# x laid out twice by the host, loaded turned ahead of and between the first weights, instead of transposed on TensorE

## The reference

```python
h = rmsnorm(x, norm_mix_g[l])                          # x: 1 x 256 x 1024
proj = jnp.einsum('bsd,dc->bsc', h, w_in[l])           # w_in: 1024 x 7168
u, v, bg, cg, xs, ga, gb = jnp.split(proj, split_at, axis=-1)
u = jax.nn.gelu(u, approximate=False)
v = rmsnorm(jax.nn.gelu(v, approximate=False), norm_v_g[l])
a = spatial_gating(u, v, w_s[l], b_s[l])
...
x = x + jnp.einsum('bsd,de->bse', m, w_out[l])
```

## Time and profile before

| | |
|---|---|
| median of 3 runs | 1056.23 us (1055.58 to 1056.95) |
| profiled execution | 1057.68 us, span 1055.9 us |
| TensorE busy | 1029.4 us, 97% |
| VectorE, ScalarE, GpSimd busy | 505.6, 408.0 and 22.2 us |
| moved by DMA | 327.89 MB, 311 GB/s over the span |

### The profile page before, as it was taken

One profiled execution on the slowest core, in us unless ns is written; L12 is line 12 of the kernel. 1 busy time (PEld: TensorE's weight loads), 2 busy tenths in 40 slices (PEclk: granted clock), 3 DMA queues, 4 the chain that ended last, 5 costly groups with the idle time before them and its releaser, 6 DMA issues.

```text
span 1055.9 us, 13811 instructions
## 1 busy us (share of the span) xinstructions
PE 1029.4 (97%) x5646; PEld 692.9 (66%) x5646; DVE 505.6 (48%) x713; ACT 408.0 (39%) x644; POOL 22.2 (2%) x42
## 2 busy tenths in 40 slices
PE   9999999999999999999999999999999999999985
PEld 6888878888999999898897544444444444434332
DVE  5676677987977755766665412121112121111112
ACT  6734634446444434664844222222222222212112
POOL 1000000010000000100000000000000000000000
PEclk9999999999999999899999999999999999999988
DMA  9977548976888653474255999999999999999992
GB/s 331 391 266 242 195 156 289 320 256 230 293 312 296 240 198 122 142 261 156 96 200 230 367 423 421 421 421 420 420 421 421 421 422 421 421 421 421 421 419 93
DMA packets 86467, 327.89 MB, mean 311 GB/s; under 512 B 5776, under 2 KB 5936, under 8 KB 61696
## 3 DMA queue, kind: packets, MB, share of 16 engines
q1 hardware_dynamic: 85056, 323.45, 79.3%
q0 software_dynamic: 1344, 3.50, 1.0%
HBM read 325.88 MB, written 1.05 MB: 310 GB/s over the span
## 4 chain that ended last, share of the span: by engine, by line
PE 48%; DMA 8%; DVE 1%; issue 1%; ACT 1%; DVEq 0%; ACTq 0%
PE bank L1025 18%; PE bank L1048 9%; PE bank L1061 3%; DMA raw<-in_w_expert_up 3%; DMA es<-in_w_expert_up 3%; PE bank L993 3%; DMA e_wlo<-in_w_expert_up 2%; PE bank L580 2%; PE bank L583 2%; PE bank L586 2%; PE bank L1034 1%; PE bank L550 1%; PE bank L556 1%; PE bank L553 1%; PE bank L1007 1%; PE bank L1009 1%
## 5 line engine op out<-in xcount | busy, mean ns | idle before, releaser
L1600 DVE TENSOR_TENSOR wlo<-raw,whi 128x2048 fp32r<-128x2048 f32 x87 | 199.0, 2290 | 95.9 <-ACT whi L1114 95.5
L1114 ACT ACTIVATE whi<-raw 128x2048 fp32r<-128x2048 f32 x87 | 165.9, 1912 | 95.9 <-PE bank L556 38.6
L2221 DVE SCALAR_TENSOR_TENSOR YS<-bank,wsl,gate2q 128x512 f32<-128x512 f32 x32 | 24.0, 751 | 217.6 <-PE bank L1048 217.6
L1025 PE MATMUL bank<-raw,XT 128*64 128x512 f32 x360 | 119.8, 597 | 0.0
L1025 PE MATMUL bank<-es,XT 128*64 128x512 f32 x328 | 113.9, 606 | 4.4 <-DMA es<-in_w_expert_up 3.4
L553 PE MATMUL bank<-wlo,hh 128*128 128x512 f32 x224 | 87.5, 391 | 1.6 <-DVE wlo L1600 1.4
L550 PE MATMUL bank<-whi,hh 128*128 128x512 f32 x224 | 88.1, 393 | 0.4 <-ACT whi L1121 0.4
L556 PE MATMUL bank<-whi,hl 128*128 128x512 f32 x224 | 87.3, 390 | 0.0
L1025 PEld LDWEIGHTS bank<-es,XT 128*64 128x64 f32 x328 | 34.2, 139 | 74.2 <-issue 73.2
L1025 PE MATMUL bank<-e_whi,XT 128*64 128x512 f32 x168 | 76.1, 596 | 2.7 <-DMA e_wlo<-in_w_expert_up 2.7
L1025 PE MATMUL bank<-e_wlo,XT 128*64 128x512 f32 x168 | 76.2, 596 | 0.0
(11 more groups left out here) (382 smaller groups left out, 1955.1 us busy)
## 6 DMA issues: line engine op xcount, KB each, us to landing
raw<-in_w_in SPq DMA_DIRECT2D x41, 1024.0 KB, 6.2
raw<-in_w_expert_up SPq DMA_DIRECT2D x33, 1024.0 KB, 22.5
raw<-in_w_ff SPq DMA_DIRECT2D x32, 1024.0 KB, 5.3
es<-in_w_expert_gate SPq DMA_DIRECT2D x31, 1024.0 KB, 22.4
raw<-in_w_ada SPq DMA_DIRECT2D x24, 1024.0 KB, 6.0
e_whi<-in_w_expert_gate SPq DMA_DIRECT2D x21, 1024.0 KB, 23.2
e_wlo<-in_w_expert_up SPq DMA_DIRECT2D x21, 1024.0 KB, 25.3
es<-in_w_expert_down SPq DMA_DIRECT2D x21, 1024.0 KB, 26.0
```

The source lines that it names most:

```text
L1025: m = e.matmul(b[64 * w:64 * w + 64, :], K.XT[j // 4 % 2][:, k, j % 4, :], K.weights(halves[w])[:, 512 * c:512 * c + 512], start=k == 0, s ...
L1114: e.activation(whi[n % RING][:, :], raw[h.raw][:, :], ACT.Copy).then_inc(S["hi"], 1)
L1600: e.tensor_tensor(wlo[n % RING][:, :], raw[h.raw][:, :], whi[n % RING][:, :].bitcast(F32), ALU.subtract).then_inc(S["lo"], 1)
```

## The change

The host lays x out a second time, turned (`xT`: 128 channels of a chunk on the partitions, then chunk, then row). SP loads it into a buffer of its own in two parts: the vectors and chunks 0 and 1 at the very beginning, chunks 2 to 7 between the two parts of half 0. The 16 transposes and the four PSUM uses go, and `hh` and `hl` are made from `xT` in SBUF. The warm-up is five matmuls of 256 columns instead of four of 512. x in its natural layout and all constants, which were loaded first, are loaded ahead of half 3, each in one transfer. TensorE still waits for all constants before half 2. The waits for `ws` and `gvb` now wait for `bgb` and `nfb` too, since all five transfers share one semaphore.

```diff
-TURNED = {"x": 0, "a": 4, ...
+TURNED = {"a": 0, "z": 4, ...
+        self.xT = slot("xT", 5, [128, 8, 256])
@@ place_psum
-        for k in range(4):
-            other(f"xT{k}", "x_lo", k + 5)
@@ pe_program
-    for _ in range(4):
-        e.matmul(bank[3][:, :], K.gate1b[:, 0:128], K.gate1b[:, 128:640], start=True, stop=True)
-    for t in range(2):
-        e.wait_ge(S[f"l_x{t}"], (32, 16)[t])
-        for k in range(4):
-            for c in range(2):
-                o, i = 256 * c + 128 * t, 512 * c + 128 * k
-                m = e.transpose(K.at[f"xT{k}"][0][:, o:o + 128], K.x[:, t, i:i + 128], C("ident"))
-            if t:
-                m.then_inc(S["turned"], 1)
+    for _ in range(5):
+        e.matmul(bank[3][:, 0:256], K.gate1b[:, 0:128], K.gate1b[:, 128:384], start=True, stop=True)
     dense("V0", 0, K.hh, K.hl, (lambda k: SPLIT["h"] + k + 1))
     e.wait_ge(S["l_cst"], 16)
     dense("V1", 2, K.hh, K.hl)
@@ mix_a on TensorE, the norm of V on VectorE
-        e.wait_ge(S["l_ws"], 48)
+        e.wait_ge(S["l_ws"], 80)
@@ act_program
     for q in range(8):
-        e.wait_ge(S["turned"], TURNED["x"] + q % 4 + 1)
-        if q > 3:
-            e.wait_ge(S["x_lo"], SPLIT["h"] + q - 3)
-        e.activation(K.hh[:, q, :], K.at[f"xT{q % 4}"][0][:, 256 * (q // 4):256 * (q // 4) + 256], ACT.Copy,
-                     scale=V("g_mix", q)).then_inc(S["x_hi"], 1)
+        e.wait_ge(S["l_xT" if q > 1 else "l_xT0"], 16)
+        e.activation(K.hh[:, q, :], K.xT[:, q, :], ACT.Copy, scale=V("g_mix", q)).then_inc(S["x_hi"], 1)
         if q < 4:
             hi_piece(0, q)
     for c in range(4):
         hi_piece(1, c)
     hi(2)
-    e.wait_ge(S["l_x0"], 32)
-    e.wait_ge(S["l_x1"], 16)
+    e.wait_ge(S["l_x"], 16)
     squares(K.x[:, 0, :], 0, K.junk3[:, 0, :])
     squares(K.x[:, 1, :], 1, K.junk3[:, 1, :])
@@ sp_program, load(h)
-            e.dma_start(K.cst[:, CW["ident"]:NCST], A["cst"][:, CW["ident"]:NCST]).then_inc(S["l_cst"], 16)
+                if c == 0:
+                    e.dma_start(K.xT[:, 2:8, :], A["xT"][:, 2:8, :]).then_inc(S["l_xT"], 16)
             return
+        if h.i == 3:
+            e.dma_start(K.x[:, :, :], A["x"][0].rearrange("(t p) n -> p t n", p=128)).then_inc(S["l_x"], 16)
+            e.dma_start(K.cst[:, :], A["cst"]).then_inc(S["l_cst"], 16)
@@ sp_program, ahead of all halves
-    e.dma_start(K.cst[:, 0:CW["ident"]], A["cst"][:, 0:CW["ident"]]).then_inc(S["l_x0"], 16)
-    e.dma_start(K.x[:, 0, :], A["x"][0, 0:128, :]).then_inc(S["l_x0"], 16)
-    e.dma_start(K.x[:, 1, :], A["x"][0, 128:256, :]).then_inc(S["l_x1"], 16)
     e.dma_start(K.vec[:, :], A["vecs"]).then_inc(S["l_vec"], 16)
+    e.dma_start(K.xT[:, 0:2, :], A["xT"][:, 0:2, :]).then_inc(S["l_xT0"], 16)
@@ lay_out, on the host
+    arrays["xT"] = np.ascontiguousarray(i["x"][0].T.reshape(8, 128, 256).transpose(1, 0, 2))
```

More of the change, by code:

```diff
@@ L47 @@
 QK, VM, OM, GT, QA, KA, VA = 0, 1024, 1536, 2048, 2056, 2568, 3080
-TURNED = {"x": 0, "a": 4, "z": 8, "b": 12, "m": 16, "f": 20, "x2": 24, "mix": 28, "x3": 32}
+TURNED = {"a": 0, "z": 4, "b": 8, "m": 12, "f": 16, "x2": 20, "mix": 24, "x3": 28}
 SPLIT = {"h": 0, "a": 8, "c": 12, "m": 16, "f": 20, "n": 28, "mx": 36}
@@ L1626, in dve_program @@
         e.wait_ge(S["x_hi"], SPLIT["h"] + q + 1)
-        e.scalar_tensor_tensor(out=K.hl[:, q, :], in0=K.at[f"xT{q % 4}"][0][:, 256 * (q // 4):256 * (q // 4) + 256],
-                               scalar=V("g_mix", q), in1=K.hh[:, q, :].bitcast(F32), op0=ALU.mult,
-                               op1=ALU.subtract).then_inc(S["x_lo"], 1)
+        e.scalar_tensor_tensor(out=K.hl[:, q, :], in0=K.xT[:, q, :], scalar=V("g_mix", q),
+                               in1=K.hh[:, q, :].bitcast(F32), op0=ALU.mult, op1=ALU.subtract).then_inc(S["x_lo"], 1)
         if q < 4:
@@ L1722, in gate_out @@
                                    op0=ALU.mult, op1=ALU.add).then_inc(S["gr"], 1)
-    e.wait_ge(S["l_bgb"], 16)
+    e.wait_ge(S["l_ws"], 80)
     gate_out("ga0", 10, K.ga, 0, 0)
@@ L1834, in dve_program @@
     e.wait_ge(S["st"], ST_AT["1"] + 2)
-    e.wait_ge(S["l_nfb"], 16)
+    e.wait_ge(S["l_ws"], 80)
     e.wait_ge(S["zl"], 16)
@@ L2315, in pool_program @@
     e.wait_ge(S["raw4"], 16)
-    e.dma_start(K.bgb[:, :], A["b_gate"].broadcast_to([128, 2048])).then_inc(S["l_bgb"], 16)
+    e.dma_start(K.bgb[:, :], A["b_gate"].broadcast_to([128, 2048])).then_inc(S["l_ws"], 16)
     e.wait_ge(S["raw5"], 16)
-    e.dma_start(K.nfb[:, :], A["norm_final_g"].broadcast_to([128, 1024])).then_inc(S["l_nfb"], 16)
+    e.dma_start(K.nfb[:, :], A["norm_final_g"].broadcast_to([128, 1024])).then_inc(S["l_ws"], 16)
     for g in range(7):
```

## The result

The changed kernel takes 1060.35 us, the median of 9 runs (1058.12 to 1065.4), against 1055.58 us of the kernel before (9 runs, 1054.3 to 1057.89). The ratio is 1.0052, with a 95% interval of 1.0041 to 1.0064. I forecast 1057.2 with a range up to 1059.3, so it is slower by 4.8 us where I had said 1.0.

A forecast was written before the change was run, and what follows sets the result against it. The prediction took TensorE's matmuls to pace the first half, with DMA full at the beginning and from about 600 us. Half 3's later landing outweighed the early start: +1.0 us on 1056.23 gave 1057.2, range 1055.3 to 1059.3.

The forecast's parts named there:

- Added: 1.049 MB: SP's load queue: x comes twice, so half 3 lands one megabyte later, 2.7 us, at 23.9 instead of 21.2.
- The constants at 21.2: SP's queue: with 5.72 MB up to their end, the constants land when half 3 did before, at 21.2 us.
- The megabyte at 392 GB/s, 2.7 us: Between constants and half 3 in SP's queue: the extra megabyte moves at 392 GB/s and takes 2.7 us.
- Half 3 on the path: ScalarE copies half 3 (1.90 us), VectorE subtracts (2.29 us); its first low product starts at 28.1, 1.0 us later.
- The second limit: ScalarE before half 3's copy: x must land for squares, table load and root, so ScalarE is free at 23.6 at best.
- The new wait for the constants: TensorE before half 2 stands until 21.2; costs nothing by itself, as half 2 ends 1.4 us ahead of 28.1.
- Halves 4 to 7: Later weight halves land 2.7 us later but have slack: half 4's low part ready at 32.5, wanted at 33.6.
- The joined semaphore: GpSimd's loads: waits for 48 become waits for 80; costed at nothing, with some 3 us of slack.
- The first product at 7 to 8: TensorE's opening: first product at 7 to 8 us instead of 9.96, a start 2 to 3 us earlier.
- A shift at 60 us reaches the end one to one: Whole program: a shift of TensorE after the first 60 us moves the end by the same amount.
- The clock rival: TensorE's clock falls in new pauses before half 2 or inside half 3; a fall costs 1.8 us, up to 1059.0; chance 0.2.
- main case: Whole kernel: +1.0 us from half 3's later low product, giving 1057.2, own range 1056.4 to 1058.2; chance 0.57.

The follow-up runs named there:

- e7_split4: The changed kernel with xT loaded as four chunks and four, not two and six: 1058.88 us against 1055.76 for the kernel before, ratio 1.004.
- e10_pool_late: The changed kernel with GpSimd's first loads (masks, gain of V's norm) behind half 3: 1055.62 us against 1055.33 for the kernel before, ratio 0.9998.
- e6_cst_wait: The changed kernel with TensorE's wait for the constants moved from ahead of half 2 to ahead of cg0: 1060.03 us against 1055.76, ratio 1.0046.
- e11_after: The changed kernel unchanged, timed again on another chip: 1059.39 us against 1055.33 for the kernel before, ratio 1.0037.
- e12_three: The kernel of e10_pool_late with nine warm-up matmuls and xT in four and four chunks: 1054.51 us against 1055.61 for the kernel before, ratio 0.9992.
- e4_after3: The changed kernel with x and constants loaded behind half 3, squares and TensorE's constants wait moved later: 1059.39 us against 1055.27, ratio 1.0037.
- e9_best: The changed kernel with several edits combined, among them x and constants behind half 4 and GpSimd's first loads behind half 3: 1056.35 us against 1055.33, ratio 1.001.
- e3_warm: The changed kernel with nine short warm-up matmuls instead of five: 1060.35 us against 1055.27 for the kernel before, ratio 1.0044.

## Why the prediction was wrong, by its steps

The mechanism was right, and its size was not. The bound of the beginning is the landing of half 3; the early start does not reach the end; the sign is that of the sum. The term that failed is in the step "Added: 1.049 MB": half 3 landed at 26.2, and I had said 23.9.

- *The constants at 21.2.* They came at 22.3 (TensorE's wait ends there). I counted bytes only, as if the engines filled equally fast with either first transfers. They moved 0.76 MB in the first 6 us (windows of 2 us: 10, 136 and 236 GB/s) and not 1.23 MB, as in the kernel before. At 390 GB/s the difference is about 1.2 us, which fits the first 1.1 us. e7_split4 gives part of it back with a larger first part in longer rows.
- *The megabyte at 392 GB/s, 2.7 us.* It took 3.9 us (22.3 to 26.2). The rate that I divided by was of all queues, and a part of it was GpSimd's: 0.40 MB of 1.57 from 22.3 to 26.3. A row that shows the real price stood in front of me: half 3 to half 4 took over 4 us in the kernel before, for one megabyte, with GpSimd's load of V's gain beside it. e10_pool_late shows whose time it was: without GpSimd's loads the constants land 2.1 us earlier and the megabyte takes 2.7 us. My argument that the masks "have passed by then" was wrong. The gain of V's norm (0.52 MB) was still moving until 24.6, and all that stands behind such loads in the queue of SP is pushed too, not only the bytes beside them. The upper bound of the sum, 3.4 us for the megabyte, was therefore too low as well.
- *Half 3 on the path.* Copy 1.92, hand over 0.03 and subtraction 2.29 us came as said: 26.27 + 4.24 = 30.5. The second limit, x and the squares, was at 23.7 (root) against 23.6 forecast, and stood behind the first.
- *The new wait for the constants costs nothing:* right, e6_cst_wait. *Halves 4 to 7 have slack:* right, there is no pause of TensorE from 31 to 60 us. *The joined semaphore costs nothing:* right, VectorE's norm of V at 43.00 has no wait. *The first product at 7 to 8:* it came at 8.54; the first xT part landed 5.3 us after its issue. The 0.43 us for a short warm-up record, which no row of the kernel before has, was near: ten records end at 6.14, not 5.9.
- *A shift at 60 us reaches the end one to one:* right to 435 us (the table). It is 3.4 us at 30 and 3.15 at 580; the last part isn't shown by the profiles.
- *The clock rival:* I gave it 0.2 as an alternative to the main case. It happens in addition to it, in some executions (two of six profiles), behind a pause of 1.8 us. I had called the pauses too short, against a row with 2.5 us. The Trainium skill, page "TensorE: Matmul & The Clock Gate", section "HAM oscillation", warns of longer pauses; the measurement decides, and here the fall came behind a pause of 1.8 us in two of six profiles.

The sum by measured terms is +3.4 us at half 3, 3.15 at 580 us, and 0.5 on average for the fall behind the pause. That makes 3.7, against medians of 4.8 and 4.1 us. What is left is up to 1.1 us. The granted clock of each execution, unprofiled ones too, says where to look for it. Its mean is 0.9881 over the changed kernel's nine executions and 0.9892 over e11_after's six, against 0.9914 to 0.9922 for the kernel before in the four sets of its executions. By an estimate from these means (what the mean lacks to 1, times the time), TensorE lost 12.6 and 11.5 us to the lower clock and not 8.3 to 9.1. In the changed kernel some 1.7 us of this lies in the opening (granted clock 0.72 from 8 to 14 us in its profile), where it costs nothing. That leaves 0.7 to 2.6 us more than in the kernel before, which take in the 0.5 above and are of the size of the rest. The profiled execution of the changed kernel, with 0.991, had the highest clock of the nine, so it hides this part. Most of the unprofiled executions lost more to the clock than this profile did. At which place they lost it, behind half 3's pause, near 440 us or in the last 50 us, isn't shown.

The gain that the new layout could have had is small in any case. Up to the end of half 0 the new order has 2.16 MB ahead and the old one had 2.23 MB, so half 0 and 1 are bound by the same loading. In e12_three nothing waits for half 3 by more than 0.2 us, and its time can't be told from that of the kernel before.

## What to carry to other kernels

Where a stretch has full DMA engines, bytes over the total rate is the price of a load only if its queue has the engines to itself (e10_pool_late: 2.7 us). Otherwise split the window by queue, or take the distance between two landings in it (3.9 us here), and look for the transfers of other queues that lie between them. A second copy of an input is not free because its reader is early: it pushes everything behind it, and in e4_after3 and e9_best moving it back by one or two halves only moved the pause. When a wait appears on TensorE, count the clock that may fall behind it as part of its price. And compare the profiled execution with the others of its kernel before you read a difference of spans.

## What the runs showed of the hardware

GpSimd's transfers of 0.39 MB of masks, part of them in rows of 256 B, and of a 0.52 MB broadcast lowered what the full DMA engines moved from 390 to 290 GB/s over some 4 us, and cost a transfer of SP's queue behind them 3.5 us. The rate was low while the masks were under way (they landed at 20.8 and 21.8 in the changed kernel) and was 391 GB/s again from 22.3, with only the broadcast left beside SP's queue. A pause of TensorE of 1.8 us was followed by a granted clock of 0.50 for 3.4 us in one execution (e3_warm) and by 1.00 in another of nearly the same kernel (the changed one); the fall made TensorE 1.6 us later at 435 us. A megabyte in SP's queue took 2.7 us with the engines to itself and 3.9 us with GpSimd's transfers beside it. Between 2 and 6 us the engines moved 136 and then 236 GB/s in the changed kernel, whose first transfers have 61 and 256 KB in rows of 2 KB or less, and 216 and then 379 GB/s in the kernel before, which has x in two transfers of 512 KB there.
